# The first expert layer of a two-block transformer: how its rows are stored and made, and when weight slots come free in both layers

## The reference, cut to what matters

```
h2  = norm(x) * (1 + scale) + shift          # scale and shift per stream: 256 tokens of x, 256 of the context
lg  = h2 @ wr_g + b_g                        # 4 groups, the best one is taken
le  = h2 @ wr_e + b_e                        # 8 experts in the group, the best two are taken
out[token] = sum over its 2 experts of weight * (silu(h2 @ w_gate[e]) * (h2 @ w_up[e])) @ w_down[e]
x   = x + gate * out
```

## Time and profile before

| | us |
|---|---|
| median of 3 runs | 3095.91 (3095.74 to 3096.76) |
| the profiled execution, its own time | 3099.11 |
| its span in the trace | 3097.8 |
| PE busy | 2687.7 (87%) |
| DVE busy | 753.8 (24%) |
| ACT busy | 482.9 (16%) |
| mean DMA rate | 222 GB/s |
| mean granted PE clock | 0.953 of full |

### The profile page before, as it was taken

The page is one execution under the profiler, slowest core; times in us unless marked ns, Lnnn a source line. Parts: engine busy times, 40 slices in busy tenths (PEclk is TensorE's granted clock), DMA queues, the critical chain, the costliest instruction groups (busy, mean ns, idle before and its releaser), DMA issues.

```text
span 3097.8 us, 56996 instructions
## 1 busy us (share of the span) xinstructions
PE 2687.7 (87%) x24517; PEld 2001.2 (65%) x24517; DVE 753.8 (24%) x2035; ACT 482.9 (16%) x1182; POOL 105.7 (3%) x146
## 2 busy tenths in 40 slices
PE   8999999999999999997997967877774998877776
PEld 7888788887888688883444545665553566544444
DVE  2003420022003420023128231111112254332223
ACT  2001310011002210012026210000001142000001
POOL 1001010011001010010000010000001000000000
PEclk9999999999999999998999989899987999999999
DMA  7544465555544465525120058789997114999997
GB/s 262 189 147 146 145 222 179 167 174 204 179 134 165 144 217 200 181 85 202 56 80 1 30 216 350 306 342 402 420 420 289 59 55 171 373 420 420 419 419 303
DMA packets 253946, 688.80 MB, mean 222 GB/s; under 512 B 15055, under 2 KB 148766, under 8 KB 237342
## 3 DMA queue, kind: packets, MB, share of 16 engines
q1 hardware_dynamic: 237184, 673.91, 57.4%
q10 hardware_dynamic: 15390, 7.48, 0.8%
q0 software_dynamic: 1152, 4.19, 0.3%
HBM read 669.95 MB, written 15.60 MB: 221 GB/s over the span
## 4 chain that ended last, share of the span: by engine, by line
PE 67%; DMA 17%; DVE 6%; issue 3%; ACT 3%; ACTq 3%; SPq 0%; POOL 0%; DVEq 0%
PE ps L663 18%; PE ps L674 10%; DMA arena<-in_moe_w_up 9%; DMA expert_out<-arena 8%; PE ps L1443 6%; PE ps L2558 3%; PE ps L1489 2%; ACTq L2270 2%; PE ps L894 2%; PE ps L687 2%; PE ps L2024 2%; PE ps L1054 2%; PE ps L2247 2%; PE ps L2519 1%; PE ps L2582 1%
## 5 line engine op out<-in xcount | busy, mean ns | idle before, releaser
L663 PE MATMUL ps<-arena 128*128 128x256 f32 x2560 | 568.6, 379 | 3.5 <-DVE arena L745 3.5
L663 PEld LDWEIGHTS ps<-arena 128*128 128x128 f32 x2560 | 483.0, 189 | 73.8 <-issue 4.1
L674 PE MATMUL ps<-arena 128*128 128x256 f32 x1408 | 317.9, 379 | 0.0
L674 PEld LDWEIGHTS ps<-arena 128*128 128x128 f32 x1408 | 264.9, 189 | 46.2 <-issue 8.4
L2232 PE MATMUL ps<-arena 128*32 128x128 f32 x6016 | 185.6, 279 | 34.6 <-issue 32.7
L2558 PE MATMUL ps<-arena 128*32 128x128 f32 x4096 | 142.4, 299 | 81.9 <-issue 80.2
L1443 PE MATMUL ps<-arena 128*128 128x512 f32 (+2 forms) x512 | 193.4, 550 | 11.2 <-ACT arena L1390 11.2
L2232 PEld LDWEIGHTS ps<-arena 128*32 128x32 f32 x6016 | 172.5, 112 | 41.6 <-issue 39.2
L787 DVE TENSOR_TENSOR arena<-arena,ps 128x256 f32<-128x256 f32 x76 | 32.1, 422 | 638.4 <-ACT arena L755 633.8
L2558 PEld LDWEIGHTS ps<-arena 128*32 128x32 f32 x4096 | 128.2, 121 | 91.0 <-issue 89.2
L1443 PEld LDWEIGHTS ps<-arena 128*128 128x128 f32 (+1 forms) x512 | 90.4, 181 | 104.4 <-issue 97.5
(11 more groups left out here) (438 smaller groups left out, 3040.2 us busy)
## 6 DMA issues: line engine op xcount, KB each, us to landing
arena<-in_moe_w_gate SPq DMA_DIRECT2D x64, 2048.0 KB, 22.0
arena<-in_moe_w_up SPq DMA_DIRECT2D x64, 2048.0 KB, 24.6
arena<-in_moe_w_down SPq DMA_DIRECT2D x64, 2048.0 KB, 29.5
arena<-in_mod_w SPq DMA_DIRECT2D x24, 2048.0 KB, 12.8
arena<-in_w_gate SPq DMA_DIRECT2D x44, 1024.0 KB, 5.3
arena<-in_w_up SPq DMA_DIRECT2D x44, 1024.0 KB, 7.9
arena<-in_w_down SPq DMA_DIRECT2D x44, 1024.0 KB, 4.8
arena<-in_w_in SPq DMA_DIRECT2D x12, 1024.0 KB, 5.6
```

What stands on the lines that cost most here:

```text
L663: last = pe.matmul(k.ps[:, T % 4, off:off + S], w[:, t, T % 2 * P:(T % 2 + 1) * P], h[:, t, :], start=(t == 0), stop=(t == KT - 1), skip_g ...
L674: last = pe.matmul(acc[:, t, :], d[:, T % 2, t * P:(t + 1) * P], k.hid[:, T % 4, :], start=(T == 0 and t % 2 == 0), stop=end, skip_group_c ...
```

## The change

In the first expert layer:

- The four stores of a block become one, of 128 partitions x 256 columns, issued one block later (behind the copy of the picked rows of the next block), out of one of two result buffers. The HBM tensor is addressed as four quarters, each of 32 rows. Everything in it lies 32 rows lower, since the first store of the loop writes a block that doesn't exist; the gathers' indices are 32 higher.
- ACT waits for the landing of the store before only ahead of the next store, no more ahead of the copy out of PSUM.
- PE turns the hidden rows before the picked rows, and DVE copies them out in this order.
- The shift is added by TensorE: the rows of a half are turned into a bank without closing the sum, and a product of the transposed root with the shift rows is added to it. ACT then takes the rows out with the scale 1/root. `pool_rows` is gone. The scaled tiles have eight buffers; tiles 0 to 3 are turned only behind the projection, tiles 4 to 6 within it.
- POOL sums the squares of tiles 0 to 6, so PE does two groups of one-column products in place of eight.

In both expert layers SP waits for the last gate and up products of an expert (`gated`, at a count that it loads from the table) before it loads into that expert's gate and up slots; only the down slot waits for `moe_ended`.

```diff
+def sp_wait_used(k, m, e, i):
+    if i == 2:
+        sp.wait_ge(*s["moe_ended"].at(l, "expert", e))
+    else:
+        if i == 0 and e == 0:
+            sp.wait_ge(*s["r_dve"].at(l, "based"))
+        if i == 0:
+            m.through = first_block(k, m, e + 1, ENG.SP)
+        sp.wait_ge(*m.step("gated", m.through, 0, 1))
...
@@ sp_experts, sp_experts_rows
-        if e >= 3:
-            sp.wait_ge(*s["moe_ended"].at(l, "expert", e - 3))
+                sp_wait_used(k, m, e - 3, i)
...
-        sp.wait_ge(*(first[ROW_SLOTS[p]] if p < 10 else s["moe_ended"].at(l, "expert", (p - 10) // 3)))
+            sp_wait_used(k, m, (p - 10) // 3, (p - 10) % 3)
...
@@ pe_token_sums
+    if i == KT - 1:
+        pe.wait_ge(*s["xs_paired"].at(KT - 2))
+        pe_square_sums(k, m.squares, False)
...
+def pool_pair_squares(k, m):
+    for i in range(1, KT - 1):
+        pool.wait_ge(*s["xs_squared"].at(i))
...
+        pool.tensor_tensor(m.squares, k.sqb[:, 0, :] if i == 1 else m.squares, k.sqb[:, i % 4, :], ALU.add)
...
+def pe_shift_half(k, m, t, half):
+    R = slice(32 * t, 32 * t + 32)
+    k.nc.tensor.matmul(k.ps[:, HALF_BANKS[t, half], :], m.rootT[R, :], m.shift_rows[R, t // 2, 512 * half:512 * half + 512], start=False, stop=True, ...)
+def pe_finish_rows(k, m):
+    pe.wait_ge(*s["xs_root"].at())
+    pe.transpose(k.ps[:, 1, 0:P], m.root, k.c["ident"]).then_inc(*s["xs_turned"].up("root"))
+    pe_turn_half(k, m, 0)
+    pe_turn_half(k, m, 1)
+    pe.wait_ge(*s["xs_row"].at())
+    pe_turn_half(k, m, 2)
+    for t, half in HALVES[:4]:
+        pe_shift_half(k, m, t, half)
+    pe.wait_ge(*s["r_dve"].at(0, "logits"))
+    pe_turn_half(k, m, 3)
+    for t, half in HALVES[4:]:
+        pe_shift_half(k, m, t, half)
...
@@ pe_experts_picked
-            pe.wait_ge(*m.step("x_out", g, 2, 1))
-            pe_turn_picked(k, m)
             pe.wait_ge(*m.step("hidden", g, 1, 1))
             pe.wait_ge(*m.step("h_ready", g, 0, 1))
             pe.transpose(ps[:, 2, 0:P], m.hb, k.c["ident"])
+            pe.wait_ge(*m.step("x_out", g, 2, 1))
+            pe_turn_picked(k, m)
...
@@ act_experts_picked
+            act_store_rows(k, m, g)
             act.wait_ge(*m.step("down", g, 1, 1))
-            act.wait_ge(*m.step("y_out", g, 0, 64))
-            act.activation(m.yb, ps[:, 3, 0:W], ACT.Copy)
-            act.wait_ge(*m.step("y_ready", g, 1, 1))
-            for q in range(4):
-                act.dma_start(k.ybuf[bass.ds(g * BL, BL), W * q:W * q + W], m.yb[BL * q:BL * q + BL, :])
+            act.activation(m.yring[:, bass.ds((g & 1) * W, W)], ps[:, 3, 0:W], ACT.Copy)
+def act_store_rows(k, m, g):
+    act.wait_ge(*m.step("y_ready", g, 0, 1))
+    act.wait_ge(*m.step("y_out", g, 0, 16))
+    act.dma_start(k.ybuf[bass.ds(g * BL, BL), :].rearrange("s (q w) -> q s w", q=4), m.yring[:, bass.ds(((g + 1) & 1) * W, W)])
```

More of the change, by code:

```diff
@@ L2098, in act_project_picked @@
                     act.wait_ge(*s["xs_prepared"].at(st, half))
[L2099 to L2107, removed]
+                    act.activation(m.shift_rows[:, st, 512 * half:512 * half + 512], ps[:, 4 + 2 * st + half, :], ACT.Copy).then_inc(*s["xs_shift"].up(st, half))
         if i == 5:
             act.activation(k.lnA[:, 0, KT:KT + 1], k.eps, ACT.Sqrt)
+    act.wait_ge(*s["xs_summed"].at())
+    act.activation(m.root.rearrange("p (t c) -> p t c", t=4)[:, :, 0], ps[:, 3, 144:148], ACT.Sqrt, scale=1.0 / D, bias=k.eps[:, 0:1]).then_inc(*s["xs_root"].up())
     act.activation(k.lnA[:, 0, KT:KT + 1], k.eps, ACT.Exp)
[L2111 to L2114, removed]
+    act.wait_ge(*s["xs_turned"].at("root"))
+    act.activation(m.rootT, ps[:, 1, 0:P], ACT.Copy).then_inc(*s["xs_row"].up())
 def dve_project_picked(k, m):
@@ L2147, in dve_picked_factors @@
         V.tensor_tensor(m.wp[:, st, :, :], m.wr, m.gains[:, st, :].unsqueeze(2).broadcast_to([P, KT, 36]), ALU.mult)
+    V.memset(m.root, 0.0)
     V.memset(m.zero, 0.0).then_inc(*r.up("factors"))
[L2151 to L2157, removed]
-        pool.tensor_tensor(row, row, permuted(m.shift_rows[:, t // 2, :], 1), ALU.add).then_inc(*s["rows_made"].up(t, 1))
-    for t in range(4):
-        pool.wait_ge(*s["xs_row"].at(t))
-        row = permuted(m.rows[:, t, :], 0)
-        pool.tensor_tensor(row, row, permuted(m.shift_rows[:, t // 2, :], 0), ALU.add).then_inc(*s["rows_made"].up(t, 0))
 def act_router_picked(k, m):
@@ L2168, in act_router_picked @@
     act.activation(m.ge, m.ge, ACT.Exp).then_inc(*s["r_act"].up(l, "group"))
-    act.wait_ge(*s["xs_out"].at(3, 0))
-    for t in range(4):
-        row = permuted(m.rows[:, t, :], 0)
-        act.activation(row, row, ACT.Copy, scale=m.r[:, t:t + 1]).then_inc(*s["xs_row"].up(t))
+    for t, half in HALVES:
+        act.wait_ge(*s["xs_shifted"].at(t, half))
+        act.activation(permuted(m.rows[:, t, :], half), k.ps[:, HALF_BANKS[t, half], :].rearrange("p (j a b) -> p b j a", j=4, b=KT), ACT.Copy,
+                       scale=m.r[:, t:t + 1]).then_inc(*s["xs_out"].up(t, half))
     act.wait_ge(*s["r_dve"].at(l, "second"))
```

81 lines of the change are left out of this document (55 added, 26 removed).

## The result

| | median, us | range | ratio to before |
|---|---|---|---|
| before | 3095.82 (4 runs) | 3092.41 to 3096.76 | |
| after | 3131.8 (4 runs) | 3129.77 to 3133.64 | 1.0111 (95%: 1.0095 to 1.0127) |

The changed kernel is 1.1% slower. Its profiled execution took 3133.64 us, its span is 3132.3 where it was 3097.8: +34.5. Lines of the code have moved: the store is L2334 (was L2270), the copy ahead of it L2325 (L2267), gate and up products L2290 (L2232), the product that ends an expert L2308 (L2250), layer 1's gate and up L2622 (L2558), SP's load L1890.

The account below looks back on a forecast made before the run. Layer 0 was taken as paced first by blocks, then by weights, layer 1 by weights alone. Terms -7.2 - 4.0 + 1.1 + 47.6 + 6.3 - 7.1 = +36.7 us gave 3135.8 profiled, 3132.6 median; range 3068 to 3185.

Parts of the forecast that it names:

- Engines of a store: Layer 0's new store: runs on four engines, 33 packets each, where the four stores before had 12 on each of 16.
- The first rival: Layer 0's store runs on 16 engines, 9 packets each, and is hidden under the blocks: 3028 us, faster; chance 15%.
- The second: Rival: four engines, but layer 0's stores lie wholly beside the weights and only capacity counts: 3071 us, faster; chance 11%.
- The loop, +47.6: Layer 0, expert 3's end to expert 31's: long stores add up on ACT, 520.7 us against 473.1, so +47.6 us.
- The slots in layer 0, counted within the loop: Layer 0's expert loop: the slot edit puts gate and up packets earlier against the stores; no separate size given.
- My third rival: Layer 0: every store meets weights, as gate and up start 5 us earlier: +120 us, about 3250; chance 8%.
- First six blocks, +1.1: Layer 0's first six blocks: three stores with weights, three without, 62.7 us against 61.6, so +1.1 us.
- Projection, -7.2: Projection: six groups of one-column products leave PE and the turns of tiles 0 to 3 move behind it, -7.2 us.
- Router and rows, -4.0: Root to first block: DVE's chain shortens without POOL, PE making the rows is the late one, 9.9 - 13.9 = -4.0 us.
- End of layer 0, +6.3: Last block to POOL in layer 0: two stores follow each other there, +6.3 us (0 to +12).
- Slots in layer 1, -7.1: Layer 1: loads start at expert 0's last gate and up product, not its end, -7.1 us (-8 to 0).
- The lower bound of the loop, -24: Layer 0's whole loop: if only the engines' capacity counts, 515 us from 1804.6, it changes by -24 us.

Follow-up runs that it names:

- e2: The changed kernel with the one store's HBM side addressed as 128 rows, so its output order differs from the reference: 3021.98 us, ratio 0.9758.
- e1: The changed kernel with each block's store as four DMAs of 32 rows again, still deferred and out of two buffers: 3031.28 us, ratio 0.9783.
- e7: The changed kernel with the slot waits of before in both layers, the store still on four engines: 3107.8 us, ratio 1.0035.
- e9: The changed kernel with the slot waits of before in layer 0 only: 3101.98 us, ratio 1.0017.
- e4: The changed kernel with layer 0's gate and up weights cut into pieces of 4 KB instead of 16 KB: 3077.38 us, ratio 0.9935.
- e3: The kernel before with only the four stores made one DMA, not deferred, one buffer: 3186.85 us, ratio 1.0287.
- e5: The kernel before with only the early freeing of gate and up slots, in both layers: 3063.74 us, ratio 0.9897.
- e6: The kernel before with only the edits to projection and rows (squares by GpSimd, shifts by TensorE): 3073.93 us, ratio 0.9927.
- e8: The changed kernel with four stores of 32 rows per block and layer 0's gate and up weights in 4 KB pieces: 3027.79 us, ratio 0.9785.

## Why the prediction was right, step by step

The time was forecast at 3133 and came at 3131.8. The main cause was the one described: a store on four engines, whose packets take turns with those of the weights. But that the number came within 1 us is luck. The loop was priced some 20 us too dear by itself, and the new slots, which cost as much there, were priced at nothing.

- **Engines of a store.** Four, with 33 packets each: 132 packets in both windows. e2 has another outer count on its HBM side and 144 packets, 16 of them closing ones, and it is faster by 110 us. The rule of the Trainium skill ("DMA: Bandwidth & Descriptors", section "Why a DMA increments its semaphore by 16 and not by 1") had this answer, and the trace agrees. The advice of the same page's table, one large transfer for many small ones, held only between two stores that are both on 16 engines: 3022.0 for one DMA (e2), 3031.3 for four (e1).
- **The first rival**, 16 engines, was priced at 3028; e1 and e2, which are that kernel, took 3031 and 3022. The price was good, the case was not this one. The second, stores wholly beside weights without a wait, is answered by the 29 distances above 12 us.
- **The loop, +47.6: +48.6.** The sum is right, its parts less so. Behind expert 3 I had 28 long stores at 15.1 to 16.0, 436 us together, and 13 short ones at 5.8 with 9 us on top, 84. The trace has 26 long distances from 1862.3 on, 417 us, and 17 short ones, 118 (together 13 more than the stretch, which they overlap at both ends): six of them are about 3.7, and many near 10, where blocks and not stores set the pace. With the new slots a long one is 16.0 in the mean. With the old ones the mean is 15.0 (e7), near the 15.1 of the sum, but it is made of some of 12.6 and others near 16. A store alone was mis-sized: 5.8 forecast, 3.65 measured. The 7.7 packets per us behind the 5.8 were read in a window that was called almost free of weights, and the same view has 72 packets of q1 in it, at 61.2% of the engines' time.
- **The slots in layer 0, counted within the loop.** This step missed. The working said that gate and up packets come "earlier against the stores", and gave that no price. e9 prices it at 29.8 us. By the profiles of the changed kernel and e7 it is 12.0 up to expert 3's end (68.7 us from the first products in the changed kernel, 56.7 in e7) and 21.1 from there on (521.6 against 500.5), some given back later. My third rival had this mechanism, gate and up just ahead of a store, at 120 us and only 8%. What covered the miss is that the loop without it was forecast too dear: 500.5 - 473.0 = +27.5 in e7, where the sum had +47.6.
- **First six blocks, +1.1: +7.2.** The same cause; in e7 this stretch is 4.9 shorter than before.
- **Projection, -7.2: -9.3** (root at 1792.00, then 1782.67). Just outside the bounds (-9 to -4). The root lies between 1777.3 and 1782.7 in eleven profiles that have the new code up to there, with a median of 1781.0, and between 1789.9 and 1792.6 in the three with the old. By the medians the step gained 11 us, so it was priced too low; which of its parts, the runs don't tell.
- **Router and rows, -4.0: -7.3** (-16.7 less -9.3), just outside its bounds (-7 to +4) too. I had PE late, with shift products at 0.87 us each (3.49 for four; the row has 3.65). Four of them took 1.14, so 0.28 each, and PE waited for ACT's row copies alone, 1.36 us ahead of the ranks. The ranks start 7.1 us behind the root (1790.08 - 1782.94), not 9.9. DVE's line of 862 ns in the earlier trace rows takes 187 now:

```profile
L1949 DVE TENSOR_TENSOR arena<-arena 128x32 f32<-128x32 f32 (+1 forms) x3 | 0.6, 187 | 0.1
L1985 DVE TENSOR_TENSOR arena<-arena 128x32 f32<-128x32 f32 x3 | 0.6, 193 | 0.1
```

- **End of layer 0, +6.3: +8.4**, two stores in a row as described. 3.3 us come back before layer 1's first products, which I did not foresee. That stretch is 264 to 265 us in after, e4 and e7, which have deferral and the long store, 266.6 in e9, which has them too, and 267 to 268 in before, e3, e5 and e6. Its cause was not tried.
- **Slots in layer 1, -7.1: -9.6 by the profiles, -5.8 by the medians of e7 and e9.** Of the 9.6, 1.5 are there without the slots (469.0 in e7). Between pairs of profiles that differ in the slots alone, this stretch shortens by 5.5 to 8.3, so the term was well sized. The first products took 3.70 us here where they took 5.42, so the first loads start earlier still.

The sum of the stages is +34.5 where I had +36.7. The lower bound of the loop, -24, doesn't follow from its own numbers (1804.6 + 515 lies 32.6 ahead of 2352.2, and 11.2 of that is the earlier start, so 21.4 would be left); it decided nothing.

## What to carry to other kernels

Before a few DMAs are made one, count on how many engines the one runs: here the outermost count of the HBM side, four quarters, left 4 of 16 and cost 100 us; keep a count such as the 32 of e1 or the 128 of e2 outermost on both sides, or keep the four DMAs. What a small transfer costs beside large ones grows with its packets per engine and with the time of one packet of the other queue (0.615 us for 16 KB, 0.164 for 4 KB here), since they took turns one by one, so look at the q-lines of a window that holds one of them. An edit that starts loads earlier is worth what it frees only while nothing on the path takes turns with those loads: it gained 32 us on the kernel before and lost 24 on the changed one. The version to keep is e1, 3031 us, 2.2% faster than before; e2's store is 9 us faster still, but no kernel was run whose gathers fit its order.

## What the hardware showed that I had not expected

- **The DMA engines idle while a store is the bound.** From 1880 to 2280 us their share is 0.81 in the changed kernel and 0.98 in e1. How much of this is twelve engines that wait for the four with the store (a load is done with its last packet), and how much are slots that come free late, was not parted. e4, with its stores on the same four engines but shorter, has 0.95.
- **Small pieces fill SP's queue.** With 4 KB pieces an issue of SP took up to 11.7 us in layer 0 and most were near 5 from 2104 us on (e4), where none took 1.5 in the changed kernel. With stores on 16 engines it costs nothing that shows: e8 has the same long issues and the time of e1.
- **Products with 32 rows are cheap side by side.** Four of 32 x 128 by 32 x 512, each in its own quarter of the rows, took 1.14 us; four of 128 x 128 by 128 x 512 took 3.65. The starts say why: the four with 32 rows start within 0.02 us of each other (1785.911 to 1785.931) and run 0.59 to 0.69 us each, those of 128 rows start one behind the other, some 0.43 us apart. So four run together, and one with 32 rows is no shorter by itself.
